# A two-block transformer layer on one core: the second block's front in three fp32r products, its attention pair by pair

## The reference

```python
z = h @ w_in                                   # 1024 -> 512 pool, 512 q, 128 k, 128 v
y_pool = pool_mixer(z[..., :512], w_pool, pool_scale)
y_attn = sliding_window_attention(q, k, v, sinks)
mix = concatenate([y_pool, y_attn]) @ w_out
h = layer_norm(ALPHA * h + mix, ln1_g, ln1_b)
ff = square(relu(h @ w_ff1)) @ w_ff2           # 1024 -> 4096 -> 1024
h = layer_norm(ALPHA * h + ff, ln2_g, ln2_b)
gate = sigmoid(h @ w_ple_gate + b_ple_gate)
h = h + gate * (p @ w_ple)
```

## Time and profile before

| what | value |
|---|---|
| median of 3 runs | 1516.47 us (1513.76 to 1516.94) |
| the profiled execution, its own time | 1516.74 us |
| its span, first to last instruction | 1515.0 us |
| busy: PE, DVE, ACT, POOL | 1430.0, 930.9, 752.2, 200.6 us |
| mean granted TensorE clock | 0.968 of full |
| second block's front, in the span | about 905 to 1111 us |

### The profile page before, as it was taken

One profiled execution on the slowest core, in us unless ns is written; L12 is line 12 of the kernel. 1 busy time (PEld: TensorE's weight loads), 2 busy tenths in 40 slices (PEclk: granted clock), 3 DMA queues, 4 the chain that ended last, 5 costly groups with the idle time before them and its releaser, 6 DMA issues.

```text
span 1515.0 us, 19584 instructions
## 1 busy us (share of the span) xinstructions
PE 1430.0 (94%) x6529; PEld 1047.6 (69%) x6530; DVE 930.9 (61%) x1129; ACT 752.2 (50%) x930; POOL 200.6 (13%) x234
## 2 busy tenths in 40 slices
PE   6899999999899999999999977988989999999998
PEld 6787667555677777777777754544468888888886
DVE  6845453354899999998989954272544413442275
ACT  4334334123699999998989840242124310333031
POOL 1011001000222222222212210041100000000010
PEclk8999999999999999999999997998989999999999
DMA  6131104315699999999999978300003321333231
GB/s 224 56 111 57 56 29 170 154 30 213 259 404 407 412 410 416 409 417 406 404 411 413 394 229 262 111 1 29 0 1 112 111 96 71 111 111 129 80 111 56
DMA packets 67892, 298.56 MB, mean 197 GB/s; under 512 B 18110, under 2 KB 20220, under 8 KB 55548
## 3 DMA queue, kind: packets, MB, share of 16 engines
q1 hardware_dynamic: 55036, 273.76, 46.6%
q10 hardware_dynamic: 7440, 15.63, 2.9%
q0 software_dynamic: 5360, 8.40, 1.7%
HBM read 292.00 MB, written 14.94 MB: 203 GB/s over the span
## 4 chain that ended last, share of the span: by engine, by line
PE 73%; DMA 6%; DVE 5%; issue 2%; ACT 2%; POOL 0%; ACTq 0%; DVEq 0%; SPq 0%; POOLq 0%
PE ps L687 12%; PE ps L869 12%; PE ps L887 11%; PE ps L725 6%; DMA ring<-in_w_gate 5%; PE ps L543 4%; PE ps L846 4%; PE ps L718 4%; PE ps L922 3%; PE ps L696 3%; PE ps L473 2%; PE ps L747 2%; PE ps L424 2%; PE ps L771 1%; PE ps L676 1%
## 5 line engine op out<-in xcount | busy, mean ns | idle before, releaser
L1940 DVE TENSOR_TENSOR ring_r<-ring,hi 128x2048 fp32r<-128x2048 f32 (+1 forms) x224 | 431.2, 1982 | 19.1 <-ACT hi L1419 17.1
L1419 ACT ACTIVATE hi<-ring 128x2048 fp32r<-128x2048 f32 (+1 forms) x224 | 363.0, 1662 | 13.3 <-DMA ring<-in_w_gate 8.3
L887 PE MATMUL ps<-ring_r,ats 128*128 128x512 f32 x768 | 174.7, 389 | 0.0
L887 PEld LDWEIGHTS ps<-ring_r,ats 128*128 128x128 f32 x768 | 144.1, 188 | 29.9
L1605 DVE TENSOR_TENSOR ring_r<-ring,ring_r 128x4096 fp32r<-128x4096 f32 x18 | 79.7, 4425 | 131.5 <-ACT ring_r L1225 131.5
L1225 ACT ACTIVATE ring_r<-ring 128x4096 fp32r<-128x4096 f32 x18 | 65.2, 3624 | 150.7 <-PE ps L887 122.0
L1088 POOL TENSOR_TENSOR rsv<-msv,half 128x1 f32<-128x1 f32 (+2 forms) x32 | 39.1, 1222 | 751.3 <-DVE msv L1565 731.4
L687 PE MATMUL ps<-ring_r,XTS 128*128 128x512 f32 x512 | 128.5, 393 | 3.9 <-DVE XTS L1945 2.1
L687 PE MATMUL ps<-hi,XTS 128*128 128x512 f32 x512 | 126.4, 389 | 0.0
L869 PE MATMUL ps<-ring_r,ring_r 128*128 128x512 f32 x512 | 123.3, 394 | 1.8 <-DVE hi L2056 1.8
L473 PE MATMUL ps<-ring_r,ring_r 128*128 128x512 f32 x448 | 117.2, 411 | 7.6 <-DVE M L1636 4.5
(11 more groups left out here) (307 smaller groups left out, 1851.7 us busy)
## 6 DMA issues: line engine op xcount, KB each, us to landing
ring<-in_w_up SPq DMA_DIRECT2D x32, 2048.0 KB, 18.4
ring<-in_w_gate SPq DMA_DIRECT2D x32, 2048.0 KB
ring<-in_w_down SPq DMA_DIRECT2D x32, 2048.0 KB, 16.9
ring<-in_w_ff SPq DMA_DIRECT2D x16, 2048.0 KB, 8.4
ring<-in_w_in SPq DMA_DIRECT2D x8, 2048.0 KB, 8.5
ring<-in_w_out SPq DMA_DIRECT2D x2, 2048.0 KB, 8.6
M<-results ACTq DMA_DIRECT2D x8, 512.0 KB, 7.5
ring<-in_w_ple_gate SPq DMA_DIRECT2D x2, 2048.0 KB, 7.8
```

What stands on the lines that cost most here:

```text
L887: ins = pe.matmul(ps[:, 2 * t + c, :], ATS[a][:, 4 * (n % 4) + k, t * P:(t + 1) * P], w[b][:, k, c * 512:(c + 1) * 512], start=(n % 4 == 0 ...
L1419: act.activation(HI[u][:, c], ring[:, s, c], ACT.Copy).then_inc(w_hi, 1)
L1940: vec.tensor_tensor(ring_r[s][:, c], ring[:, s, c], HI[u][:, c].bitcast(F32), ALU.subtract).then_inc(w_lo, 1)
```

## The change

- q2, kv2, pool2, mix0 and mix1 are split like the feed-forward units, each in two halves (`part_hi` on ScalarE, `part_lo` on VectorE; kv2's halves are 1024 wide, the others 2048). The feed-forward and gate units are split in two halves too, instead of one instruction of 4096 each. The tops lie in slots 0 and 1, at the places of `hi_at`.
- The turned X is split (tops by ScalarE for both halves, rests by VectorE in `x3_rest`, between the tiles of the addition), as are the mix inputs: `MIXH` and `MIXL_POOL`, `MIXL_ATT`.
- Every weight product of the front is three fp32r ones (`piece`; 24 for a 128-column group). V is computed channel by channel like K and turned by four transposes ("vt").
- Attention runs pair by pair: j, i = divmod(n, 4). Ahead of the loop stand K, pair 0 of q and V; the other three pairs of q are in steps 0, 1 and 2, and pool2 is spread over steps 3 to 15, channel group 3 first. The four pool outputs are in steps 13, 16, 18 and behind the loop. POOL takes window 16 first. Scores use three banks in rotation instead of four, the outputs banks 7 and 5.
- All UNITS_2 use slots 2, 3, 4: pool2 waits for the last expert's down weights and the gathered results, mix0 for q2's last product, mix1 for kv2's, up0 for pool2's.
- The eight result reads are issued by ScalarE (four) and SP (four, after a signal of POOL).
- One short VectorE instruction in `biased` is dropped (negated sinks are made once). In the mix, k runs over 4, 5, 6, 7, 3, 2, 1, 0.

```diff
+SPLIT_2 = UNITS_2
+FILLS_2 = [[("q2", n + 1, 0, 24)] if n < 3 else [] for n in range(16)]
+U2_STEPS = [96 * n // 13 for n in range(14)]
+for n in range(13):
+    for q, c in enumerate((3, 2, 1, 0)):
+        a, b = max(U2_STEPS[n], 24 * q), min(U2_STEPS[n + 1], 24 * q + 24)
+        if a < b:
+            FILLS_2[3 + n].append(("pool2", c, a - 24 * q, b - 24 * q))
+U2_ENDS = {c: n for n in range(16) for u, c, a, b in FILLS_2[n] if u == "pool2" and b == 24}
+PW_AT = {3: 13, 2: 16, 1: 18}
+PASSES = ((0, 0), (1, 0), (0, 1))
...
+            s = RAW_SLOTS[(n + 1) % len(RAW_SLOTS)]
...
+        hi_at = {"q2": (0, HALF), "kv2": (2 * HALF, 2 * HALF + HALF // 2), "pool2": (3 * HALF, 0)}
+        for n, u in enumerate(SPLIT_2[3:]):
+            hi_at[u] = (0, 3 * HALF) if n % 2 else (HALF, 2 * HALF)
...
+            def piece(u, c, m0, m1):
+
+                j, key = SPLIT_2.index(u), (u, c)
+                width = 2 * P if u == "kv2" else 512
+                if m0 == 0:
+                    open_turn(pe, key, jobs[0] % 2)
+                    jobs[0] += 1
+                bank = turn[key][0]
+                for q in range(m0, m1):
+                    p, r = divmod(q, 12)
+                    i, k = r // 4, 4 * p + r % 4
+                    if r == 0 and c == (3 if u == "pool2" else 0):
+                        pe.wait_ge(w2_hi, 2 * j + p + 1)
+                        pe.wait_ge(w2_lo, 2 * j + p + 1)
+                    w = weight(u, PASSES[i][0], k * width + c * P, P)
+                    ins = pe.matmul(ps[:, bank, :], w, HTS[PASSES[i][1]][:, k, :], start=(q == 0), stop=(q == 23))
+                if m1 == 24:
+                    fill_turn(ins, key)
+                    last_turn[u] = key
...
+                j, i = divmod(n, TT)
                 lo = P if i == 0 else 0
+                if n == 0:
+                    left(pe, ("kv2", 0))
+                if i == 0:
+                    left(pe, ("q2", j))
                 for a in range(2):
                     r = slice(a * QK, (a + 1) * QK)
-                    o = open_turn(pe, ("S2", n, a), 2 + 2 * (n % 2) + a)
+                    o = open_turn(pe, ("S2", n, a), 2 + (2 * n + a) % 3)
...
+            def pool_out(g):
+                pe.wait_ge(pool_ready, 4 - g)
+                o = open_turn(pe, ("pw", g), jobs[0] % 2)
+                jobs[0] += 1
+                fill_turn(pe.matmul(o, WP2[:, g, :], DP[:, g, :], start=True, stop=True), ("pw", g))
+
+            piece("kv2", 0, 0, 24)
+            piece("q2", 0, 0, 24)
+            piece("kv2", 1, 0, 24)
+            pe.wait_ge(wp_in, 16)
             for n in range(19):
+                if n == 1:
+                    left(pe, ("kv2", 1))
+                    transposes("vt", jobs[0] % 2, VT, TT)
+                    jobs[0] += 1
...
-                    pooled(n)
+                    for work in FILLS_2[n]:
+                        piece(*work)
...
+                for g, at in PW_AT.items():
+                    if at == n:
+                        pool_out(g)
+            pool_out(0)
...
+                    for q, k in enumerate((4, 5, 6, 7, 3, 2, 1, 0)):
+                        if c == 0 and t == 0:
+                            left(pe, ("O2", k - 4) if k >= 4 else ("pw", k))
+                        mix = (MIXH[:, k, t * P:(t + 1) * P],
+                               (MIXL_ATT[:, k - 4, :] if k >= 4 else MIXL_POOL[:, k, :])[:, t * P:(t + 1) * P])
+                        for i, (a, b) in enumerate(PASSES):
+                            ins = pe.matmul(o, mix[b], weight(u, a, k * 512, 512), start=(q == 0 and i == 0),
+                                            stop=(q == DT - 1 and i == 2))
...
+                if n < 3:
+                    if n == 2:
+                        sp.wait_ge(results_in, 1)
+                        for t in range(TT):
+                            sp.dma_start(YG[:, 1, t, :], results[T + t * P:T + (t + 1) * P, :]).then_inc(yg_in[t], 16)
                         sp.wait_ge(yg_in[TT - 1], 32)
-                    freed(NE - 2 + n // 3, n % 3)
+                    freed(NE - 2 + n // 2, n)
...
+            until(pool, y_out, blocks * 16 + 16)
+            until(pool, rows_in, blocks * 16 + 32)
+            pool.memset(BEGUN, 0.0).then_inc(results_in, 1)
...
+            def part_hi(j, p):
+                u = SPLIT_2[j]
+                s, loads = place[u]
+                if p == 0:
+                    act.wait_ge(slot_in[s], loads)
+                if (j, p) in ((2, 1), (3, 0)):
+                    used_up(act, "q2")
+                elif (j, p) == (3, 1):
+                    used_up(act, "kv2")
+                elif (j, p) == (4, 0):
+                    used_up(act, "pool2")
+                elif j >= 5 and p == 0:
+                    used_up(act, SPLIT_2[j - 2])
+                a = p * part_size(u)
+                act.activation(hi_of(u, a, part_size(u)), ring[:, s, a:a + part_size(u)], ACT.Copy).then_inc(w2_hi, 1)
+
+            part_hi(0, 0)
+            part_hi(0, 1)
             act.wait_ge(y_out, blocks * 16 + 16)
             act.wait_ge(rows_in, blocks * 16 + 32)
             for t in range(TT):
-                for k in range(2):
-                    act.dma_start(YG[:, k, t, :], results[k * T + t * P:k * T + (t + 1) * P, :]).then_inc(yg_in[t], 16)
+                act.dma_start(YG[:, 0, t, :], results[t * P:(t + 1) * P, :]).then_inc(yg_in[t], 16)
+            act.wait_ge(up_raw_used, blocks)
+            part_hi(1, 0)
+            part_hi(1, 1)
...
+            part_hi(2, 0)
+            leave(act.activation(K2, filled(act, ("kv2", 0)), ACT.Copy), ("kv2", 0))
+            leave(act.activation(Q2[:, 0, :], filled(act, ("q2", 0)), ACT.Copy), ("q2", 0))
+            leave(act.activation(VT, filled(act, ("kv2", 1)), ACT.Copy), ("kv2", 1))
...
+                if n < 3:
+                    leave(act.activation(Q2[:, n + 1, :], filled(act, ("q2", n + 1)), ACT.Copy), ("q2", n + 1))
+                if n == 1:
+                    leave(act.activation(V2, filled(act, "vt").rearrange("p (t d) -> p t d", t=TT), ACT.Copy), "vt")
+                for c, at in U2_ENDS.items():
+                    if at == n:
+                        leave(act.activation(U2[:, c, :], filled(act, ("pool2", c)), ACT.Copy), ("pool2", c))
+                if n in (3, 7, 9):
+                    part_hi(*{3: (2, 1), 7: (3, 0), 9: (3, 1)}[n])
...
+            def part_lo(j, p):
+                u = SPLIT_2[j]
+                s, a, n = place[u][0], p * part_size(u), part_size(u)
+                vec.wait_ge(w2_hi, 2 * j + p + 1)
+                vec.tensor_tensor(ring_r[s][:, a:a + n], ring[:, s, a:a + n], hi_of(u, a, n).bitcast(F32),
+                                  ALU.subtract).then_inc(w2_lo, 1)
+
+            def x3_rest(t):
+                for c in range(2):
+                    vec.wait_ge(x3_hi, 2 * t + c + 1)
+                    a = (slice(None), slice(4 * c, 4 * c + 4), slice(t * P, (t + 1) * P))
+                    leave(vec.tensor_tensor(HTS[1][a], filled(vec, ("x3", t, c)).rearrange("p (k t) -> p k t", k=4),
+                                            HTS[0][a].bitcast(F32), ALU.subtract), ("x3", t, c))
+
+            part_lo(0, 0)
+            part_lo(0, 1)
...
+                if t == 0:
+                    part_lo(1, 0)
+                    part_lo(1, 1)
+                else:
+                    x3_rest(t - 1)
+            x3_rest(TT - 1)
...
-                step(vec.tensor_tensor(st[:, b:b + 2], st[:, b:b + 2], snk, ALU.max))
-                step(vec.tensor_scalar(st[:, b + 2:b + 4], st[:, b:b + 2], -1.0, None, ALU.mult))
-                vec.tensor_tensor(st[:, b + 6:b + 8], snk, st[:, b:b + 2], ALU.subtract).then_inc(nmax2, 1)
+                step(vec.scalar_tensor_tensor(out=st[:, b + 2:b + 4], in0=st[:, b:b + 2], scalar=-1.0, in1=nsnk,
+                                              op0=ALU.mult, op1=ALU.min))
+                vec.tensor_tensor(st[:, b + 6:b + 8], snk, st[:, b + 2:b + 4], ALU.add).then_inc(nmax2, 1)
...
                     biased(n)
-                if n:
+                if 1 <= n <= 16:
                     probabilities(n - 1)
+                if n in (4, 8, 10):
+                    part_lo(*{4: (2, 1), 8: (3, 0), 10: (3, 1)}[n])
+                if n >= 6 and (n - 6) % 4 == 0:
+                    j = (n - 6) // 4
+                    vec.wait_ge(att_hi, j + 1)
+                    leave(vec.tensor_tensor(MIXL_ATT[:, j, :], filled(vec, ("O2", j)), MIXH[:, 4 + j, :].bitcast(F32),
+                                            ALU.subtract), ("O2", j))
+                for g, at in PW_AT.items():
+                    if at == n:
+                        pool_rest(g)
+            pool_rest(0)
+            part_lo(4, 0)
+            part_lo(4, 1)
 
```

More of the change, by code:

```diff
@@ L741, in _ @@
                 left(pe, ("x3", t, 1))
-            w = unit(pe, "q2").rearrange("p (k c) -> p k c", k=DT)
-            for n in range(PAIRS):
```

(16 more changed lines are left out.)

191 lines of the change are left out of this document (74 added, 117 removed).

## The result

The changed kernel takes 1498.81 us in the median of 4 runs (1497.15 to 1501.27), the kernel before, beside it, 1516.43 (1513.76 to 1516.94): a ratio of 0.989, 95% interval 0.987 to 0.991. It is faster by 17.6 us where 25.8 were forecast. The profiled execution took 1497.15, its span is 1495.4.

The account below looks back on a forecast made before the run. TensorE led the chain before; VectorE was to set loop steps 3 to 14. Mix at 1028.0 plus 57.6 put the first up product at 1085.6, 25.9 us earlier: 1490.7 us, own range 1486 to 1497, wider range 1481 to 1504.

Parts of the forecast that it names:

- Gather and residual: From gathered results to first product: kv2's and the tiles' rests on VectorE delay it to 929.8, a loss of 3.6 us.
- Loop start and its first steps: Attention loop starts at 948.3; steps 0 to 2 each carry 16.3 us of q products, so step 3 starts at 967.5.
- Steps 3 to 14: Attention loop's filled part: VectorE, not TensorE, sets it, at 49.0 us including 2.4 of idle time.
- TensorE sets the loop: Rival: POOL's interference falls into VectorE's waits, steps 3 to 14 take 43.1 us; 1485 in all, chance 0.2.
- The clock falls for part of it: Rival: TensorE's clock drops for four steps of the attention loop, adding 10 us; 1501 in all, chance 0.17.
- The clock falls for all of it: Rival: half clock through twelve loop steps, 78 us for 49; 1520 in all, chance 0.03.
- the products don't get cheaper: Rival: loading each weight three times binds, leaving little but the removed waits; 1513 in all, chance 0.02.
- POOL's lock: Shared-port rule: the loop's three weight rests on VectorE each wait for or hold up POOL, up to 4.5 us more.
- The sum by the short rows: POOL's work beside VectorE in steps 3 to 14 slows it 0.28 for each us, 5.6 us over 20 us.
- End of the loop and mix: Behind step 15's scores: mix starts at 1028.0, first up product 57.6 us later, VectorE setting the pace after mix0.
- Weights: Mix0's load lands at 983, 2 us before its split in step 7; if late, 0 to 4 us.

Follow-up runs that it names:

- e8: Changed kernel with pool2's second half split early, attention and pool rests a step later, probability copy before the exponentials, kv2's rests before the gathered tiles: 1484.77 us.
- e2: Changed kernel with POOL's windowed sums cut to one column, so nothing of POOL runs beside VectorE: 1491.03 us.
- e1: Changed kernel with pool2's second half split in steps 0 and 1, before the loop needs it: 1497.54 us, loop 87.2 for 89.0.
- e3: Changed kernel with the rests of attention and pool outputs one step later on VectorE: 1493.66 us, loop 84.3 for 89.0.
- e10: e8 with ScalarE's order as in the changed kernel, the probability copy again behind the exponentials: 1487.42 us, loop 82.5.
- e9: e8 with mix0's two rests cut into four quarters over steps 8 to 11: median 1483.82 us, 0.979 of the kernel before; loop 75.3.
- e7: Changed kernel with 60 of pool2's 96 products left out: 1499.75 us, loop 90.5 for 89.0.
- e13: e9 with 60 of pool2's 96 products left out: 1479.37 us, loop 73.7 for 75.3.
- e6: Changed kernel with ScalarE's copy of older probabilities moved ahead of each step's exponentials: 1500.13 us, loop 90.7 for 89.0.
- e11: Changed kernel with the norm behind the mix taking statistics over only the first 512 columns of each tile: first mix to first up product 55.8 us for 57.4.

## Why the prediction was right or wrong

**Gather and residual: right.** First product at 926.24 against 926.8; the loss against before, by the experts' last copy, is 3.0 us where 3.6 was given. VectorE in the kernel after, rows that answer to the earlier trace rows:

```profile
907.58 1.28 DVE L2049 SCALAR_TENSOR_TENSOR X<-M,wts,X 128x1024 f32<-128x1024 f32 x1 [2.75 <-DMA M<-results]
908.90 1.28 DVE L2051 SCALAR_TENSOR_TENSOR X<-M,wts,X 128x1024 f32<-128x1024 f32 x1
910.10 2.36 DVE L2034 TENSOR_TENSOR ring_r<-ring,ring_two 128x1024 fp32r<-128x1024 f32 x2
912.37 1.28 DVE L2049 SCALAR_TENSOR_TENSOR X<-M,wts,X 128x1024 f32<-128x1024 f32 x1
```

kv2's rests stand in the path as said, and the split issue didn't bring tile 0 forward (907.58 is 910.57 less the 3.0). e8 shows that this placement costs 2.0 us.

**Loop start and its first steps: right.** 945.55 against 945.3, and three steps of 6.6 on average, from scores to scores, against 6.4. (The text says that two more pairs of q no longer stand ahead of the loop. It is three, and its sum has all three: 16.3 us for 72 records.) A record of the unbroken pieces takes 0.236 (5.67 / 24) where 0.2267 was taken.

**Steps 3 to 14: wrong, and this is the whole miss.** The text took 31.3 + 6.9 + 2.8 + 5.6 us of VectorE's work and 2.4 of idle time. The work was right: 59.2 less the waits is 46.8, against 46.6. Its parts too: POOL 5.3 (e2). The idle time of 2.18 in step 4 came as given, though e1 shows that it isn't the stop's, and TensorE's stop there took 2.36 us where 4.0 stood in the text. The step that failed is the sentence that VectorE sets this part and so hardly waits. It waited 12.4 us, not 2.4, because a step isn't a stream into VectorE but a circle through four queues. The text added VectorE's new pieces as if the other engines would work on beneath them. Each was instead placed in front of the next step's maxima, for which ScalarE, and behind it TensorE, stood still. e3, e8, e10 and e9 show it: with the computation unchanged, order and size of pieces alone take the stretch from 59.2 to 46.1, below even the 49.0 that was forecast. (Part of that is pool2's second rest, 2.3 us of VectorE's work that e1's edit takes out of the stretch.) Two of the prediction's own signs tell the same: a loop longer than 85 us (it was 89.0), and VectorE almost without idle time in these steps (15.7 us of 59.2 not busy).

**The rivals.** *TensorE sets the loop* (43.1): no in this kernel (e7); in e9 its 46.1 us come near to it, yet e13 shows VectorE as the limit there. *The clock falls for part of it* (1501): this is partly what happened, and the marker named for it, a clock below 0.9 from 970 to 1015, was just met with 0.89. By e2's records the lowered clock kept TensorE busy 4.0 us longer, but little of that reaches the end of the stretch: in e2, at full clock, 9.1 of the 10.2 missing us are still there. It came with the stops: in e6 they are 2.95 and 3.22 us, and the windows that hold them have 0.68 and 0.66. e9's stretch is as long at 1.00 as at 0.96. The Trainium skill ("TensorE: Matmul & The Clock Gate", HAM oscillation) says that waits between bursts of products keep the clock low. By that rule a long stop and a low clock go together, and e6's rows agree; how long a wait it takes, no run here shows. *The clock falls for all of it* and *the products don't get cheaper*: no; 96 mix products' worth is 21.82 us, 0.227 for each record.

**POOL's lock.** The row at 1001.72 shows 3.12 us for a rest that takes 2.29 in e2, 0.83 more, and beside it POOL's 8-column instruction with 2.13 us, where such an instruction takes 0.20 to 0.22 otherwise (0.21 in e9 timed). The Trainium skill ("SBUF — State Buffer", SBUF: two separate sides) has one of the two block the other for a whole instruction; the trace agrees that both sides are held up. But only one of the loop's three rests met POOL's work (the other two took 2.28 and 2.29 us), so that the loss was 0.8 us and not the 4.5 that the text gave by that rule. The sum by the short rows, 5.6 us for all of POOL's work, holds without that rule.

**End of the loop and mix: right.** Step 15's scores to the mix 9.9 us (10.8 said). Mix to first up product 56.8 by the chain (57.4 from the first mix record's own start), 57.6 said. VectorE's first and last tiles in the kernel after:

```profile
1063.42 0.68 DVE L2124 SCALAR_TENSOR_TENSOR X<-X,ps 128x512 f32<-128x512 f32 x1
...
1075.75 0.68 DVE L2124 SCALAR_TENSOR_TENSOR X<-X,ps 128x512 f32<-128x512 f32 x1
...
1082.50 0.68 DVE L2124 SCALAR_TENSOR_TENSOR X<-X,ps 128x512 f32<-128x512 f32 x1
```

It is free 28.3 us after the mix's start (28.6 said) and a later tile takes 6.75 (6.9 said); of 11.7 us saved on TensorE 9.3 arrive. VectorE keeps the rest: none of these rows has a wait for a product, and e11's shorter statistics bring the end forward.

**Weights: right.** Mix0's two tops ran at 989.11 and 998.71 without a wait of ScalarE.

**The number.** The miss of 9.4 us at the first up product, less the 3.0 us by which this execution's experts were faster, makes 6.3 in the profiled span; the median is 8.1 us above the forecast of 1490.7. The range held the time. The forecast's own range (1486 to 1497) didn't. That the wider one did is luck in part: its upper end of 1504 was there for a lowered clock, and the waits that made up most of the miss stood in no term.

## What to carry to other kernels

A loop in which engines hand one step to each other takes neither the longest busy sum nor the sum of all: where it hops, size it by following one step through every queue, with each new piece of work at its place in its engine's order, and ask which later step's first instruction stands behind it. Put extra pieces behind whatever the other engines wait for, never directly behind a value of the same step, and cut them to the slack of one step. And judge such edits together: one by one they gave 1.8, 4.7, -1.7 and 0.9 us, while the set gave 13.7. Two of them simply added; the copy's place and the quarters paid only once the other waits were gone.

## What was not expected

- Leaving out 13.6 us of TensorE's work made the changed kernel's loop 1.5 us longer (e7), with the granted clock at 0.82 instead of 0.91 over steps 3 to 15. Lighter load there meant a lower clock and no earlier end.
- POOL slows more of VectorE's instructions than the prediction counted. The two-column L2085 (1.04 us where it otherwise takes 0.16) was known from the earlier trace rows; but L2095 too, which reads one tile and a column of scales, took 1.40 us for two where two take 0.62 with POOL idle:

```profile
986.27 1.04 DVE L2085 SCALAR_TENSOR_TENSOR st<-st 128x2 f32<-128x2 f32 x1
...
987.81 1.40 DVE L2095 TENSOR_SCALAR M<-M,st 128x256 f32<-128x256 f32 x2
...
1008.20 0.62 DVE L2095 TENSOR_SCALAR M<-M,st 128x256 f32<-128x256 f32 x2
```

- One edit changed its sign with its surroundings: the copy ahead of the exponential cost 1.7 us alone (e6, at a lower clock) and gained 3.3 with the others in place (e8 against e10, at the same clock).

What stays open is whether POOL's windowed sums could run elsewhere than beside VectorE; e2 left them out rather than moved them, so the 5.3 us are a bound and not a gain that was shown.
